# Attention of a hybrid decoder step: exponentials split in two as the stationary side, their remainders computed by POOL

## The chip, the core and the metric

One core of one Trainium2 chip runs the whole program. The metric is the device time of one execution in microseconds (us).

## The reference

The program is one inference step of a two-layer decoder, for a prompt of 2048 rows and for 8 decode rows with 4096 rows of paged cache each. All of it is fp32. Layer 0 (gated MLP and a linear recurrence) is not touched by the change. Layer 1 is forgetting attention with 16 heads of 64:

```python
q, k_p, v_p, g, logf_p = _fox_project(yp, norm1_g, w_in1, fox_b_f, q_norm_g, k_norm_g)
att = _fox_prompt_attention(q, k_p, v_p, logf_p)
yp = yp + (att * jax.nn.silu(g)) @ w_out1
...
s = jnp.einsum('bqhd,bkhd->bhqk', q_i, k) * ATTN_SCALE
s = s + cq_i[..., :, None] - ck[:, :, None, :]
p = jax.nn.softmax(jnp.where(mask, s, -jnp.inf), axis=-1)
return jnp.einsum('bhqk,bkhd->bqhd', p, v)
```

`_fox_sample_attention` does the same for the decode rows over the paged keys and values.

## The kernel before

The program is a row of stages: setup, norm and layer 0 (to about 745 us), the output projection of layer 0, `project1` (about 1024 to 1880), `past`, `attention` (about 1921 to 3225) and `out1` (from about 3239). In each stage every engine has its own instruction list, and semaphores tie them together. An F32R matmul is PE's one-pass form of fp32 and sees a rounded operand; a product that must keep fp32 is made of a rounded high part and the remainder, in three such matmuls (`split3`, L112 to L114).

**`project1`** makes q, k, v and g of the prompt in 128 units (16 column chunks of 256 in the order q, k, v, g, times 8 row pairs; `unit`, 48 matmuls of 256 columns). q and k are squared on ACT (L1373), normed on DVE (L1541, for k also L1549) and transposed by PE (`turn`, L1241, four 128x128 per unit), since attention wants them by feature; g goes through Silu and is transposed too. `turn(n - 1)` stands behind `unit(n)` in PE's list. v and k also go to DRAM by rows. Beside that POOL and DVE make the scores of the decode rows with the paged keys (L1151, L1564; `p_kp` a page, `p_qb` the query row spread over partitions).

**`attention`** works by units: a head times a chunk of 512 queries, c = 0 to 3. Unit c has 4(c+1) blocks of 128 keys; a block is a *step*, 40 steps a head, 640 in all. A Python function, `schedule`, writes the order; the loop body is a pair of heads, one decode row's attention rides on each pair. The kinds of work in that order are:

- `M` (L1953, on the diagonal L1956): one product of 128 queries by up to 512 keys, rounded, into one of two PSUM banks; DVE takes its row maxima (L2076). `MN` (L2080) joins them, `MR` (L1963) turns them into a row by four transposes, and ACT writes that row into Q2 (L2046), where it acts as the 65th feature.
- `QK`: the scores of one step, 128 keys by up to 512 queries, as two matmuls (L1975 with high and low parts of q stacked, L1977) and the mask on the diagonal (L1980). ACT takes the exponential into `W` (L2040).
- `PV` (L1990), two steps behind: `V` (128 keys by 65, the last column ones) is stationary and `W` moves, in fp32, into one bank `O` of 65 by 512.
- `OE`: DVE multiplies `O` by the gate (L2086), ACT copies the 65th row, the sum of the exponentials (L2051), and POOL stores both (L1920, L1922); the sum is divided out only in `out1`.
- `SD` to `VC`: the decode row. `SD` (L2092, L2093) begins it; `VG` (L2016) are eight groups of four V pages, on the odd head of each pair, the pages loaded by SP two groups ahead.
- `LD`: ten loads of the next head; a memset on POOL (L1929) puts the ones row into Q2.

PE's waits around the change read, in the order of a step:

```python
pe.wait_ge(ex, NS * i + max(0, n - 1))
...
pe.wait_ge(ex, NS * i + n + 1)
if kb == 0:
    pe.wait_ge(oed, 2 * NC * i + u)
    pe.wait_ge(oea, 2 * NC * i + u)
nc.tensor.matmul(O[0:HR, P * j:512], V[s][:, kb, :], W[n % 3][:, 0:512 - P * j],
```

**`out1`** multiplies 17 tiles of rows with the output weights by `split3`. For each tile it inverts the sums, spreads them over the features of each head by 16 matmuls (L2282) and multiplies (L2239) before it splits the result (L2215, L2246).

Of the kernel before, what the change touches and what calls it, by code (L numbers as in the profile page):

```python
# [965 lines left out]
def project1(nc, z, a, C, xh, xl, D, out):  # L966
# [22 lines left out]
    def turn_no(n):  # L989
        return count("qkg", n)  # L990
# [4 lines left out]
    def rows_stored(n):  # L995

        return 16 * slots("kv", n, lambda m: m)
# [14 lines left out]
    with ExitStack() as ctx:  # L1012
# [57 lines left out]
        def _(sp):  # L1070
# [66 lines left out]
            for x in range(2):  # L1137
                sp.wait_ge(scst[x], 16 * (B // 2))
                sp.wait_ge(hst[x], 16 * (count("qkg", N) // 2))
                sp.wait_ge(lst[x], 16 * (count("qk", N) // 2))  # L1140
                sp.wait_ge(rst[x], 16 * (count("kv", N) // 2))
# [12 lines left out]
        def _(pe):  # L1154
# [67 lines left out]
            def turn(n):  # L1222
# [4 lines left out]
                elif kind == "k":  # L1227
                    pe.wait_ge(kgained, count("k", n + 1))
                else:
                    pe.wait_ge(vfree, count("vg", n + 1))  # L1230
                if x >= 2:
                    pe.wait_ge(hid, x - 1)
                    before = [m for m in range(n) if UNITS[m][2] in "qkg" and turn_no(m) == x - 2][0]
                    pe.wait_ge(lod, low_no(before + 1))
# [19 lines left out]
            for n in range(N):  # L1254
# [9 lines left out]
            turn(N - 1)  # L1264

        @block.scalar
        def _(act):
# [22 lines left out]
            def hi(n):  # L1290
# [4 lines left out]
                if kind == "g":  # L1295
                    nc.scalar.activation(hi_t[:, x % 2].bitcast(F32), tp[x % 2][:], ACT.Copy).then_inc(hid, 1)
                else:
                    nc.scalar.activation(hi_t[:, x % 2], tp[x % 2][:], ACT.Copy, scale=C.qg[:] if kind == "q" else 1.0).then_inc(hid, 1)

            def store_hi(n):  # L1300
# [4 lines left out]
                dst = {"q": D.qh, "k": D.kh, "g": D.sg}[kind]  # L1305
# [12 lines left out]
            def store_rows(n):  # L1318
# [4 lines left out]
                else:  # L1323
                    act.wait_ge(vfree, count("vg", n + 1))
                act.dma_start(out[kind + "_prompt"][0, CWD * u:CWD * u + CWD, HC * i:HC * i + HC, :].rearrange("(t r) h d -> r t (h d)", r=P),
                              rows[:, n % 2]).then_inc(rst[n % 2], 16)
# [37 lines left out]
            for n in range(N):  # L1364
                c, u, kind = UNITS[n]
                if n >= 2 and UNITS[n - 2][2] in "qk":
                    store_lo(n - 2)
                if n and UNITS[n - 1][2] in "kv":
# [10 lines left out]
                if n and UNITS[n - 1][2] != "v":  # L1379
                    hi(n - 1)  # L1380
# [3 lines left out]
                if n and UNITS[n - 1][2] != "v":  # L1384
                    store_hi(n - 1)
# [3 lines left out]
            hi(N - 1)  # L1389
            store_hi(N - 1)  # L1390

        @block.vector
        def _(dve):
# [130 lines left out]
            for n in range(N):  # L1524
# [5 lines left out]
                if n and UNITS[n - 1][2] in "qk":  # L1530
                    lo(n - 1)
# [138 lines left out]

# [720 lines left out]
```

## Time and profile before

| | us |
|---|---|
| median of 3 runs (lowest to highest) | 3478.22 (3470.8 to 3479.21) |
| the profiled execution, its own time | 3480.33 |
| its span, first to last instruction | 3478.7 |
| PE busy | 3017.1 (87%) |
| DVE busy | 1533.7 (44%) |
| ACT busy | 1032.3 (30%) |
| POOL busy | 761.5 (22%) |
| mean granted TensorE clock, share of full speed | 0.935 |
| DMA | 547.04 MB in 323904 packets |

The profile is one execution. An engine's busy time is the sum of its instructions; PE's matmuls are pipelined and their ends modelled, so starts are safer to read than ends. "Idle before" is what an engine stood still ahead of an instruction, and behind the arrow stands what released it. Lines are those of the kernel before.

### The profile page before, as it was taken

To read this page: it belongs to the slowest core of one execution; us is meant where nothing else is said; L and a number is where in the kernel's file an instruction comes from. 1 tells how busy PE (TensorE), PEld (TensorE's weight loads), DVE (VectorE), ACT (ScalarE), POOL (GpSimd) and SP (SyncE) were. 2 spreads that over 40 slices of the span, in tenths; PEclk is the share of its full clock that TensorE was granted. 3 is DMA by queue.
4 is the path that set the end of the run, shared out by engine and by line. 5 is a ranking of instruction groups with operands and counts; after the bars stand their busy time and mean duration, and the time that the engine had idled before them with its cause. 6 is when DMAs were issued, how large, how long until landed. Compare 5 with 4: busy or idle time off the path is not lost. (4 is left out here: it accounts for less than half of the span.)

```text
span 3478.7 us, 48124 instructions
## 1 busy us (share of the span) xinstructions
PE 3017.1 (87%) x17005; PEld 2320.1 (67%) x17005; DVE 1533.7 (44%) x2068; ACT 1032.3 (30%) x1711; POOL 761.5 (22%) x475
## 2 busy tenths in 40 slices
PE   3879797959989999989996689898989889899799
PEld 3869696947759999989886445454545445454687
DVE  5132323233557667685775334343424333342332
ACT  5222223232452122221211234343434343343100
POOL 0000000010004886878765200000100000000000
PEclk9989898979989999999998799999999999999899
DMA  3111000035636888888785765748475757654442
GB/s 113 32 35 39 25 30 25 24 101 178 184 115 210 271 267 276 265 260 269 252 271 159 167 183 137 205 114 250 99 228 127 215 150 200 173 143 152 149 127 68
DMA packets 323904, 547.04 MB, mean 157 GB/s; under 512 B 77309, under 2 KB 221345, under 8 KB 314220
## 3 DMA queue, kind: packets, MB, share of 16 engines
q1 hardware_dynamic: 220172, 445.81, 42.8%
q10 hardware_dynamic: 95424, 75.61, 7.6%
q0 software_dynamic: 8128, 23.33, 2.1%
q8 instruction: 98, 1.61, 0.2%
q14 instruction: 82, 0.67, 0.1%
HBM read 449.58 MB, written 95.12 MB: 157 GB/s over the span
## 5 line engine op out<-in xcount | busy, mean ns | idle before, releaser
L1151 POOL TENSOR_TENSOR p_kp<-p_kp,p_qb 128x1024 f32<-128x1024 f32 x256 | 625.7, 2471 | 385.7 <-DMA p_kp<-in_cache_k_dram 314.0
L2076 DVE TENSOR_REDUCE at_mx<-at_mx 128x1 f32<-128x512 f32 (+3 forms) x640 | 379.9, 608 | 718.3 <-PE at_mx L1953 475.7
L2040 ACT ACTIVATE at_w<-at_st,c_nckt 128x512 f32<-128x512 f32 (+3 forms) x640 | 397.3, 623 | 690.9 <-PE at_st L1977 380.2
L1990 PE MATMUL at_o<-at_w,at_v 128*65 128x512 f32 (+3 forms) x1280 | 578.0, 535 | 17.0 <-DVE at_og L2086 8.0
L112 PE MATMUL p_pb<-p_w,x_xh 128*128 128x256 f32 x2048 | 591.8, 289 | 0.7 <-DVE p_w L1462 0.7
L113 PE MATMUL p_pb<-p_w,x_xh 128*128 128x256 f32 x2048 | 579.1, 283 | 0.0
L114 PE MATMUL p_pb<-p_w,x_xl 128*128 128x256 f32 x2048 | 578.6, 283 | 0.0
L1975 PE MATMUL at_st<-at_q,at_k 128*128 128x512 f32 (+3 forms) x640 | 407.4, 637 | 4.4 <-ACT at_w L2040 4.4
L1564 DVE TENSOR_REDUCE p_sc<-p_kp 128x16 f32<-128x1024 f32 x256 | 307.5, 1214 | 217.6 <-POOL p_kp L1151 217.3
L112 PEld LDWEIGHTS p_pb<-p_w,x_xh 128*128 128x128 f32 x2048 | 390.5, 191 | 12.1 <-issue 11.2
L113 PEld LDWEIGHTS p_pb<-p_w,x_xh 128*128 128x128 f32 x2048 | 391.9, 191 | 0.0
L114 PEld LDWEIGHTS p_pb<-p_w,x_xl 128*128 128x128 f32 x2048 | 391.2, 191 | 0.0
L112 PE MATMUL l_pb<-x_xh,l_wh 128*128 128x412 f32 x800 | 289.1, 361 | 73.1 <-DVE l_wl L857 73.1
L1920 POOL DMA_DIRECT2D att<-at_og x64 | 34.5, 539 | 1187.2 <-DVE at_og L2086 928.8
L113 PE MATMUL l_pb<-x_xl,l_wh 128*128 128x412 f32 x800 | 285.8, 357 | 0.0
L114 PE MATMUL l_pb<-x_xh,l_wl 128*128 128x412 f32 x800 | 285.3, 357 | 0.0
L1953 PE MATMUL at_mx<-at_km,at_q 65*128 65x512 f32 (+3 forms) x640 | 245.5, 402 | 35.5 <-DMA at_k<-kl 29.8
L112 PE MATMUL o_pp<-o_wh,o_mh 128*128 128x512 f32 (+1 forms) x544 | 220.7, 406 | 33.1 <-DVE o_wl L586 22.7
L1975 PEld LDWEIGHTS at_st<-at_q,at_k 128*128 128x128 f32 x640 | 122.9, 192 | 179.1 <-issue 152.9
L1977 PE MATMUL at_st<-at_q,at_k 65*128 65x512 f32 (+3 forms) x640 | 237.5, 371 | 0.0
L2016 PE MATMUL at_cv<-at_vp,at_sw 128*32 128x512 f32 x1056 | 154.1, 663 | 82.9 <-DMA at_vp<-in_cache_v_dram 82.9
L113 PE MATMUL o_pp<-o_wl,o_mh 128*128 128x512 f32 (+1 forms) x544 | 216.2, 397 | 0.0
(289 smaller groups left out, 3880.4 us busy)
## 6 DMA issues: line engine op xcount, KB each, us to landing
p_kp<-in_cache_k_dram SPq DMA_DIRECT2D x256, 512.0 KB, 4.9
at_vp<-in_cache_v_dram SPq DMA_DIRECT2D x256, 512.0 KB, 5.6
o_mt<-mixed SPq DMA_DIRECT2D x32, 512.0 KB, 5.1
p_raw<-in_w_in_dram SPq DMA_DIRECT2D x32, 512.0 KB, 6.9
at_q<-qh SPq DMA_DIRECT2D x32, 512.0 KB
at_k<-kh SPq DMA_DIRECT2D x32, 512.0 KB
l_raw<-in_w_in_dram SPq DMA_DIRECT2D x20, 512.0 KB
mixed<-l_w POOLq DMA_DIRECT2D x8, 1028.0 KB, 4.2
```

Source lines behind the costliest of these rows:

```text
L112: nc.tensor.matmul(out, lhs[0], rhs[0], start=(k == 0), stop=False)
L113: nc.tensor.matmul(out, lhs[0], rhs[1], start=False, stop=False)
L114: return nc.tensor.matmul(out, lhs[1], rhs[0], start=False, stop=(k == nk - 1))
L1151: nc.gpsimd.tensor_tensor(kp[:, g % 4], kp[:, g % 4], qb[:], ALU.mult).then_inc(kmul, 1)
L1564: nc.vector.tensor_reduce(sc[:, b % 2].rearrange("p (h g) -> p h g", g=z.PG)[:, :, r], by_head(kp[:, g % 4], z.H), AX.X, ALU.add).then_inc ...
L1953: last = nc.tensor.matmul(MX[m % 2][:, 0:wd], Q2[s][0:HR, t * P:(t + 1) * P], KM[s][0:HR, seg * 512:seg * 512 + wd], start=True, stop=seg < c)
L1975: nc.tensor.matmul(ST[n % 2][:, 0:wd], K1[s][:, ks], Q1[s][:, q0:q0 + wd], start=True, stop=False)
L1977: last = nc.tensor.matmul(ST[n % 2][:, 0:wd], K2[s][:, ks], Q2[s][:, q0:q0 + wd], start=False, stop=not diagonal)
L1990: nc.tensor.matmul(O[0:HR, P * j:512], V[s][:, kb, :], W[n % 3][:, 0:512 - P * j], start=(kb == 0), stop=(kb == 4 * c + 3)).then_inc(pv, 1)
L2016: last = nc.tensor.matmul(CV[32 * g:32 * g + 32, half, :], sw[:, 4 * r + g, :], src[:, 512 * half:512 * half + 512], start=(r == 0), stop= ...
L2040: nc.scalar.activation(W[n % 3][:, 0:wd], ST[n % 2][:, 0:wd], ACT.Exp, bias=C.nckt[:, kb, ds(2 * i + u // NC, 1)]).then_inc(ex, 1)
L2076: nc.vector.reduce_max(mx[:, u % 2, j, seg:seg + 1], MX[m % 2][:, 0:wd], AX.X).then_inc(mread, 1)
```

## The change

1. `project1`: g is stored by rows like k and v, without transposes. The transposes of q and k stand two units behind the products, not one, and with them ACT's high part, DVE's low part and their stores.
2. `attention` is written out in full, with no loop over pairs. The exponentials `W` are rounded by ACT into `Wh` (step kind `RD`), and POOL computes every remainder `Wl` = `W` - `Wh` (`WL`; `low_on_dve` is always false). For each 128 queries `Wh` and then `Wl` are the stationary side, and V moves: 130 columns (high part 64, ones 2, low part 64) for `Wh`, 66 for `Wl`. `O` is now 128 queries by 2 banks of 260 columns, opened by a matmul with zeros. `PV` is three steps behind, and held for two steps at the start of a unit. V is split once a head, high part on ACT, low part on POOL (`VS`). `MR` uses a bank of the two of `M`. `OE` comes in two halves, after the PV of block 4c+1 and of the last: DVE inverts the sum, scales by it and the gate, and adds the two parts. The gate is loaded and the result stored for each unit, by rows, on SP's queue.
3. `out1`: the sums, their inverses, the 16 matmuls and the multiply go; each tile is turned by 8 transposes.

```diff
@@ project1 @@
-                if n and UNITS[n - 1][2] != "v":
-                    turn(n - 1)
+                if n >= 2 and UNITS[n - 2][2] in "qk":
+                    turn(n - 2)
...
@@ attention, the order @@
+                if n >= 2:
+                    seq.append(("WL", n - 2))
+                pending.append((u, kb, n))
+                if hold:
+                    hold -= 1
+                while len(pending) > LAG and not (hold and pending[0][1] == 0):
+                    p = pending.pop(0)
+                    weigh(p)
+                    if p[1] == blocks(p[0]) - 1:
+                        hold = 2
...
@@ attention, PE @@
-                        nc.tensor.matmul(O[0:HR, P * j:512], V[s][:, kb, :], W[n % 3][:, 0:512 - P * j],
-                                         start=(kb == 0), stop=(kb == 4 * c + 3)).then_inc(pv, 1)
...
+                    for jj in range(j, 4):
+                        if kb == 0 and u and jj % 2 == 0:
+                            pe.wait_ge(osc, 2 * u - 1 + jj // 2)
+                        if kb == 0 and jj % 2 == 0:
+                            nc.tensor.matmul(O[:, jj // 2, 0:2 * VW], identr[0:1, :], zero[:], start=True, stop=False)
+                        q = slice(P * (jj - j), P * (jj - j + 1))
+                        nc.tensor.matmul(o_tile(jj, ALL), Wh[n % RH][:, q], V[s][:, kb, ALL], start=False, stop=False)
+                        last = nc.tensor.matmul(o_tile(jj, FRONT), Wl[n % RH][:, q], V[s][:, kb, FRONT], start=False,
+                                                stop=jj % 2 == 1 and kb == 4 * c + jj)
...
@@ attention, ACT @@
+            value_high(0)
+            value_high(1)
...
+                elif w[0] == "RD":
+                    n = w[1]
+                    wd = width(n)
+                    act.wait_ge(ex, n + 1)
+                    if n >= RH:
+                        act.wait_ge(pv, n - RH + 1)
+                    nc.scalar.activation(Wh[n % RH][:, 0:wd], W[n % RW][:, 0:wd], ACT.Copy).then_inc(rdd, 1)
...
@@ attention, POOL @@
+                if w[0] == "WL" and not low_on_dve(w[1]):
+                    n = w[1]
+                    wd = width(n)
+                    pool.wait_ge(rdd, n + 1)
+                    nc.gpsimd.tensor_tensor(Wl[n % RH][:, 0:wd], W[n % RW][:, 0:wd], Wh[n % RH][:, 0:wd].bitcast(F32), ALU.subtract).then_inc(wlp, 1)
...
@@ attention, DVE @@
-                        nc.vector.tensor_tensor(og[u % 2][0:HD, :], O[0:HD, :], SG[s][:, 512 * c:512 * c + 512], ALU.mult).then_inc(oed, 1)
...
+                    nc.vector.reciprocal(ol[:, u % 2, 2 * half:2 * half + 2], one).then_inc(old, 1)
...
+                    for part, dst in ((HI, oa), (LO, ob)):
+                        for j in js:
+                            last = nc.vector.scalar_tensor_tensor(out=dst[:, j, :], in0=o_tile(j, part), scalar=ol[:, u % 2, j:j + 1],
+                                                                  in1=SG[u % 2][:, j, :], op0=ALU.mult, op1=ALU.mult)
+                    last.then_inc(osc, 1)
...
+                    nc.vector.tensor_tensor(og[u % 2][:, 2 * half:2 * half + 2, :], oa[:, 2 * half:2 * half + 2, :],
+                                            ob[:, 2 * half:2 * half + 2, :], ALU.add).then_inc(oadd, 1)
...
@@ out1, PE @@
-                    last = nc.tensor.matmul(rb[:, n % 2, k, 0:rows], expand[:, k * P:(k + 1) * P], rl[:, ds(col, rows)],
-                                            start=True, stop=True)
+                    last = nc.tensor.transpose(tp[:, n % 2, k, :], mt[:, n % 3, k * P:(k + 1) * P], C.ident[:])
```

How the order of the instructions moves, first on PE at the end of a short unit (`at_st` scores, `at_mx` products for maxima, `at_o` the output). Before:

```order
L1990 MATMUL at_o<-at_w,at_v 65x256
L1975 MATMUL at_st<-at_q_0,at_k_0 128x512
L1977 MATMUL at_st<-at_q_0,at_k_0 128x512
L1953 MATMUL at_mx<-at_km,at_q_0 128x512 x2
L1956 MATMUL at_mx<-at_maskr,at_identr 128x128
L1990 MATMUL at_o<-at_w,at_v 65x128
```

After, from the last PV but one of the unit:

```order
L2063 MATMUL at_o<-at_v,at_wh 128x130
L2064 MATMUL at_o<-at_v,at_wl 128x66
L2039 MATMUL at_st<-at_q_0,at_k_0 128x512
L2041 MATMUL at_st<-at_q_0,at_k_0 128x512
L2017 MATMUL at_mx<-at_km,at_q_0 128x384
L2020 MATMUL at_mx<-at_maskr,at_identr 128x128
L2039 MATMUL at_st<-at_q_0,at_k_0 128x512
L2041 MATMUL at_st<-at_q_0,at_k_0 128x512
L2017 MATMUL at_mx<-at_km,at_q_0 128x512
L2061 MATMUL at_o<-at_zero,at_identr 128x260
```

Between the last PV of a unit and the first of the next there are now two QKs and no PV; the matmul with zeros opens the new sum. On DVE, at the start of a head (`at_mx` the maxima, `at_sd` the decode row's scores, `at_o` the output), before:

```order
L2092 TENSOR_TENSOR at_sd<-at_sc,c_decay 128x16x32
L2093 ISA
L2093 TENSOR_TENSOR at_sd<-at_sn,c_decay 128x16
L2075 REGISTER_ALU
L2076 TENSOR_REDUCE at_mx<-at_mx 128x1
```

and after:

```order
L2148 TENSOR_REDUCE at_mx<-at_mx 128x1 x2
L2186 TENSOR_TENSOR at_sd<-at_sc,c_decay 128x16x32
L2187 TENSOR_TENSOR at_sd<-at_sn,c_decay 128x16
L2148 TENSOR_REDUCE at_mx<-at_mx 128x1 x2
L2166 RECIPROCAL at_ol<-at_o 128x2
L2172 SCALAR_TENSOR_TENSOR at_oa<-at_o,at_ol,at_sg 128x64 x2
L2172 SCALAR_TENSOR_TENSOR at_ob<-at_o,at_ol,at_sg 128x64 x2
L2178 TENSOR_TENSOR at_og<-at_oa,at_ob 128x128
```

Where one multiply per unit stood in DVE's list among four or more reduces, there is now, twice per unit, a reciprocal, four scaled multiplies and an add.

## Rows read from the trace of the kernel before

**Rows 1.** Windows of the span: project1 and attention; the first line names the columns.
```profile
core 0: us, PE busy (x) PEld busy (x) DVE busy (x) ACT busy (x) POOL busy (x), PEclk, DMA share, GB/s
1037.00:1880.00 843.00, 799.10 (x6671) 779.22 (x6670) 576.15 (x657) 189.18 (x334) 625.72 (x256) 0.97 0.80 256
1960.00:3224.00 1264.00, 1153.94 (x5167) 626.35 (x5165) 469.06 (x850) 481.82 (x776) 90.69 (x140) 0.95 0.61 169
```

**Rows 2.** Timeline of PE in a full step: start, us, engine, line, operation.
```profile
2501.31 0.79 PE L1975 MATMUL at_st<-at_q,at_k 128*128 128x512 f32 x1
2502.17 1.02 PE L1990 MATMUL at_o<-at_w,at_v 128*65 128x512 f32 x2
2502.63 0.80 PE L1975 MATMUL at_st<-at_q,at_k 128*128 128x512 f32 x1
```

**Rows 3.** The same windows for one pair of heads; 2123.8 begins the even head.
```profile
2123.80:2142.40 18.60, 17.55 (x66) 11.05 (x64) 12.04 (x22) 7.25 (x12) 3.87 (x5) 0.82 0.70 162
2124.00:2194.00 70.00, 68.26 (x284) 40.67 (x284) 33.44 (x62) 31.96 (x52) 5.95 (x9) 0.95 0.38 84
2128.00:2133.00 5.00, 5.00 (x13) 2.76 (x12) 2.53 (x6) 0.37 (x1) 0.52 (x1) 0.50 0.65 154
2194.00:2287.00 93.00, 79.73 (x371) 39.58 (x370) 26.56 (x48) 28.65 (x47) 5.95 (x9) 0.93 0.81 234
```

**Rows 4.** Costliest groups of the page, the V pages of the decode rows.
```profile
L2016 PE MATMUL at_cv<-at_vp,at_sw 128*32 128x512 f32 x1056 | 154.1, 663 | 82.9 <-DMA at_vp<-in_cache_v_dram 82.9
```

**Rows 5.** Groups of attention by line and form: ACT's exponential, DVE's reduce.
```profile
L2040 ACT ACTIVATE at_w<-at_st,c_nckt 128x512 f32<-128x512 f32 x448 | 307.0, 687 | 501.2 <-PE at_st L1977 380.2 <-PE at_st L1980 74.3 <-issue 44.6
L2076 DVE TENSOR_REDUCE at_mx<-at_mx 128x1 f32<-128x512 f32 x448 | 302.6, 687 | 518.0 <-PE at_mx L1953 475.7 <-PE at_mx L1956 41.9
```

**Rows 6.** Timeline of PE in project1, one unit's four transposes.
```profile
1870.13 0.60 PE L1241 MATMUL p_tp<-c_ident,p_rows 128*128 128x128 f32 x4
1870.48 0.36 PE L112 MATMUL p_pb<-p_w,x_xh 128*128 128x256 f32 x1
1870.69 0.28 PE L113 MATMUL p_pb<-p_w,x_xh 128*128 128x256 f32 x1
1870.81 0.28 PE L114 MATMUL p_pb<-p_w,x_xl 128*128 128x256 f32 x1
```

**Rows 7.** The transposes' line L1241 in project1: what ended PE's idle time, us, times.
```profile
  DVE p_rows L1541: 45.8, 10
  DVE p_rows L1549: 33.0, 25
```

**Rows 8.** Timeline of project1 at the longest of these waits, in brackets idle time and releaser.
```profile
1481.21 2.34 POOL L1151 TENSOR_TENSOR p_kp<-p_kp,p_qb 128x1024 f32<-128x1024 f32 x1 [11.70 <-DMA p_qb<-qs]
1486.95 1.11 PE L1241 MATMUL p_tp<-c_ident,p_rows 128*128 128x128 f32 x4 [10.29 <-DVE p_rows L1541]
```

**Rows 9.** Chain that ended last, one tile of out1.
```profile
3265.94 1.98 PE o_rb L2282 x16
```

**Rows 10.** Timeline at the start of attention, ACT's first exponential.
```profile
1961.66 1.28 ACT L2040 ACT_TABLE_LOAD   x1 [0.41 <-PE at_st L1980]
```

**Rows 11.** Timeline of PE, sixteen loads with one column each.
```profile
3217.50 1.84 PE L2023 MATMUL at_cv<-c_onescol,at_cm 128*128 128x1 f32 x16
```

**Rows 12.** POOL's lines L1151 and L1929: duration ns min/median/max.
```profile
L1151 POOL TENSOR_TENSOR p_kp<-p_kp,p_qb x256: 2337/2397/3426, 1046.8 to 1871.0; 128x1024 f32<-128x1024 f32 x128
L1929 POOL MEMSET at_q<- x14: 1797/1799/1801, 2031.9 to 3086.7; 1x2048 f32 x14
```

**Rows 13.** ACT's rounding copy of 128x512 in out1, L2225.
```profile
L2225 ACT ACTIVATE o_wh<-o_raw x16: 612/630/634, 3245.4 to 3258.6; 128x512 fp32r<-128x512 f32 x16
```

**Rows 14.** DVE's lines L1541 (from PSUM), L1549 (from SBUF), and four small ones.
```profile
L1541 DVE TENSOR_TENSOR p_rows<-p_pb,p_rs x64: 690/691/693, 1040.7 to 1781.5; 128x512 f32<-128x512 f32 x64
L1549 DVE TENSOR_TENSOR p_rows<-p_rows,p_kgb x32: 691/1098/2896, 1092.2 to 1782.2; 128x512 f32<-128x512 f32 x32
20.31 1.01 DVE L201 TENSOR_SCALAR c_w<-c_ident,su_w 8x8 f32<-8x8 f32 x4
```

More of the change, by code:

```diff
@@ L1680, in attention, with blocks, first_step, width @@
     HR = HD + 1
-    NS = 2 * sum(4 * (c + 1) for c in range(NC))
-    NLD = 10
+    U = H * NC
+    HB = 2 * (NC * (NC + 1))
+    N = HB * H
+    NLD = 8
     VG = PG // 4
-    VI = PG // 4 + 1
+    VW = 2 * HD + 2
+    LAG = 3
+    RW, RH = 4, 5
+    def blocks(u):
+        return 4 * (u % NC + 1)
+    def first_step(u):
+        return HB * (u // NC) + sum(blocks(x) for x in range(u % NC))
+    def width(n):
+        u = max(x for x in range(NC * (n // HB), NC * (n // HB) + NC) if first_step(x) <= n)
+        kb = n - first_step(u)
+        return 512 - P * max(0, kb - 4 * (u % NC))
@@ L1685, in attention @@
+    SEQ = schedule()
+    RING = [w for w in SEQ if w[0] in ("M", "MR")]
     with ExitStack() as ctx:
@@ L1875, in _ @@
-            run(0, schedule(False), True, False)
-            with sp.Fori(1, B - 1) as i:
-                run(i, schedule(False), False, False)
-            run(B - 1, schedule(True), False, True)
+            due = []
+            for w in SEQ:
+                if w[0] == "LD":
+                    head_load(w[1], w[2])
+                elif w[0] == "LV":
+                    value_load(w[1])
+                elif w[0] == "OE" and w[2] == 1:
+                    due.append([3, w[1]])
+                elif w[0] == "SD" and w[-1] < B - 1:
+                    sp.wait_ge(sdd, 2 * w[-1] + 2)
+                    scores(w[-1] + 1)
+                elif w[0] == "VG":
+                    values(w[-1], w[1])
+                elif w[0] == "VN":
+                    values(w[-1], VG)
+                elif w[0] == "QK":
+                    for d in due:
+                        d[0] -= 1
+                    while due and due[0][0] <= 0:
+                        u = due.pop(0)[1]
+                        store(u)
+                        if u + 2 < U:
+                            gate_load(u + 2)
@@ L1880, in _ @@
+            for _, u in due:
+                store(u)
             sp.wait_ge(fin, 2)
-            sp.dma_start(D.att[:, T:TS].rearrange("(k p) b -> p k b", p=P), atts[:]).then_inc(fst, 16)
-            sp.dma_start(D.lsum[:, T:TS], ones[:]).then_inc(fst, 16)
-            sp.wait_ge(fst, 32)
+            sp.dma_start(D.atts.rearrange("(k p) b -> p k b", p=P), atts[:]).then_inc(fst, 16)
+            sp.wait_ge(fst, 16)
+            for x in range(2):
+                sp.wait_ge(ogst[x], 16 * (U // 2))
@@ L1885, in _ @@
         @block.gpsimd
         def _(pool):
-            nc.gpsimd.memset(sw[:], 0.0).then_inc(made, 1)
+            for s in range(2):
+                nc.gpsimd.memset(K2[s][HD:HR].bitcast(F32), 1.0).then_inc(made, 1)
+                nc.gpsimd.memset(Q2[s][HD:HR].bitcast(F32), 1.0).then_inc(onesd, 1)
+            pool.wait_ge(made, 2)
+            pool.wait_ge(onesd, 2)
+            nc.gpsimd.memset(zero[:].bitcast(F32), 0.0).then_inc(made, 1)
+            pool.wait_ge(made, 3)
             nc.gpsimd.memset(sn[:], 0.0).then_inc(snz, 1)
@@ L2159, in out1, with by_feature @@
         block = ctx.enter_context(nc.Block())
+        def by_feature(n, rows):
+            return tp[:, n % 2, :, :] if rows == P else ms[:]
         @block.sync
```

770 lines of the change are left out of this document (390 added, 380 removed).

## The prediction

> **What bounds the kernel now.** I read the table of windows first. Attention, from 1960 to 3224 us, is 1264 us of the span, and PE is busy in 1154 of them, DVE in 469, ACT in 482 and POOL in 91 [rows 1]: PE is the engine that the others feed. Its timeline shows a full step without a product as QK, QK, PV, one step every 1.32 us (2501.31 to 2502.63) [rows 2]. 256 columns take 0.12 us in a dense stretch [rows 6], so the two score matmuls of 512 columns take 0.43 to 0.48 and leave about 0.87 to PV's 512 columns in fp32, which is four cycles a column at 2.4 GHz. PE has no gap there. The windows of one pair of heads say where it has: the even head takes 70 us (2124 to 2194), the odd one 93 us [rows 3]; the odd one holds the V pages of the decode rows, where PE sat 82.9 us idle over all eight pairs until pages landed [rows 4]. The first eight steps of the even head take 18.6 us, 5 of them at a clock of 0.50, the 1.2 GHz level, after PE had stopped again and again for DVE's reduces [rows 3]. ACT and DVE need 687 ns each for a 128x512 piece, half a step [rows 5].
>
> **`project1`.** The gate's units are no longer transposed: 32 units of four transposes go. The timeline has four of them at 1870.13 and the products behind them at 1870.48, 1870.69 and 1870.81; products are 0.12 apart otherwise, so they took 0.35 + 0.09, say 0.45 us per unit [rows 6], and 32 x 0.45 = 14.4 us. The other part is the lag. Transposes of q and k now stand two units behind instead of one. PE sat idle 45.8 and 33.0 us, 79 together, before transposes until DVE's normed rows were there [rows 7]. One more unit is 48 matmuls x 0.118 = 5.7 us of cover. That covers all of the short waits; the longest is 10.29 us, from a query row that landed late (POOL waited 11.70 us for it, DVE waits for POOL, PE for DVE) [rows 8], and keeps some 4.6 us. Some waits also move to the next thing that DVE is late with, since its work is the same: of 79 I take 43, with ends of 16 and 79. The sum is -57, ends -30 and -93. The order of the loads and stores moves by one unit of 5.7 us and nothing waits for the gate's stores; that is priced at nothing.
>
> **`out1`.** Sixteen expand matmuls per tile take 1.98 us on the chain, 15 times alike, and more at the first tile [rows 9]. Eight 128x128 transposes take their place: at 0.11 a piece 0.9, say 0.98. 16 x 1.0 = 16, and 2 more for the reciprocals and the divide ahead of the first tile: -18, ends -12 and -20.
>
> **Start of attention.** ACT now rounds V of heads 0 and 1 ahead of its first exponential, and V(1) stands on SP's queue behind about 12.5 MB. Before, ACT turned to its first exponential at 1961.66 [rows 10]. From about 1920, 12.5 MB at 256 GB/s end at 1969, at 169 GB/s at 1994 [rows 1]. With the first QK waiting for ACT's maxima row too, this is +15, ends +3 and +35.
>
> **Attention, PE.** Per 128x128 block of weights there are now two loads and matmuls of 130 and 66 columns. Sixteen loads with a single column took 1.84 us, 0.115 each [rows 11]; that is load-bound, and 130 or 66 columns fit under it. 2 x 2176 of them plus 128 zeroing ones, at 0.111 (between 0.107, 256 columns' time, and that 0.115), are 497 us. What goes is 278,528 columns x 4 cycles = 464 us. So PE gains nothing from one-pass arithmetic: +33, ends +15 and +51.
>
> **Attention, POOL.** 640 remainders. No row has a 512-wide one; nearest is the two-input TENSOR_TENSOR of 128x1024 at 2337 ns [rows 12]: half is 1.17, the whole 2.34. I take 1.3. A head is then 28 x 1.3 + 4 x (1.0 + 0.7 + 0.4) + 4.2 = 49 us, under its PE work (58); at 2.34 it would be 84 a head and POOL the bound. The chain exponential 0.69, rounding 0.63 [rows 5, 13], remainder 1.3 and 0.3 of semaphores is 2.9 us, and a lag of three steps gives 4.5: hidden in full steps. Once a head POOL also splits V's low part (2.4 us, the row's own price for 1024 elements) while ACT rounds the high part (1.1): 3.5, less the 1.6 of slack, is 1.9 x 14 = +27, ends 0 and +49. The memset of the ones row (1.80 us [rows 12]) stands before the first steps' remainders and is covered: POOL is ahead there, since DVE holds the start; without that cover it costs 25.
>
> **Attention, DVE.** It gives up one multiply per unit and gets two halves of an evacuation: a reciprocal 0.16, four scaled multiplies 128x64 at 0.23 (four small ones follow each other in 1.01 us [rows 14]), a wait on itself 0.1, an add of two SBUF tiles 0.3, and 0.4 for what POOL does to such an add: a DVE add from PSUM took 690 to 693 ns whatever POOL did, one from SBUF 691 to 2896 with a median of 1098 [rows 14]. 1.9 each, 128 of them. Where does that matter? In the first eight steps of a head sixteen reduces (10.0) and four halves are 17.6 us against 10.8 before; 18.6 passed there with DVE busy in 12.0 [rows 3]. Between 0 (it fits the 6.6 idle) and 6.8 (in series) I take 5, because reduces and PE's products alternate on two banks: 16 x 5 = +80, ends 0 and +109. At the change to units c=2 and c=3, four steps hold 6.3 and 5.8 us of DVE against 3.9 and 4.3 of PE, so +3.9 x 16 = +62, ends 0 and +62. The queued reduces wait behind the halves, and PE waits for both: its next products, and its first PV into O.
>
> **What absorbs it.** The 82.9 us of page waits [rows 4] are in the odd heads; a slower head gives pages time. About half of what I add lies there, (33 + 27 + 80 + 62)/2 = 101, more than the waits, so most of them go, but not all lie where the delay does: -70, ends 0 and -83. Attention nets 33 + 27 + 80 + 62 - 70 = +132.
>
> **Sum.** 3480.3 of the profiled execution (2 above the median of the runs, inside their spread) - 57 - 18 + 15 + 132 = 3552.3.
>
> **Rivals.** *Everything new is hidden.* DVE's halves fit its idle time, POOL keeps ahead: what remains is PE's 33 with half absorbed and a start of 3. 3480 - 57 - 18 + 3 + 17 = 3425. For it: DVE is busy in 37% of attention [rows 1]. Against: the start of a head, where that share was 12.0 of 18.6. *Near cancel*: half of the new waits, 3480. *The clock falls.* In the first steps of a head it was 0.50 for 5 us [rows 3]; with more stops there and at unit changes the mean of attention could go from 0.95 to 0.85: 65 us a head x (1/0.85 - 1/0.95 = 0.124) = 8, x 15 to 16 heads = +120: 3672. It decides from when PE's stops double.
>
> *Loads in series.* If a short matmul did not cover the next load, each of the 2176 pairs would cost its 196 columns, 0.0815 us, more: +177, 3729. The rows speak against: pairs of a 128-wide load and 256 columns follow each other 0.12 us apart [rows 6], less than load plus matmul. The Trainium skill, page "TensorE: Matmul & The Clock Gate", Part 3, "What overlaps and what doesn't", says that a load overlaps a matmul in flight only where their row groups differ, which here they don't. By that rule this rival would be the forecast; the trace disagrees with its 0.12.
>
> **How the numbers follow.** Chances: the forecast 0.54, all hidden 0.26, near cancel 0.05, clock 0.12, loads in series 0.03. A measurement of this kernel can tell about 0.3%, 10 us. Faster comes from the hidden case, same from the cancel, slower from the rest. Range: the hidden case with a better lag (-20) to the clock case and the forecast with its DVE and PE terms at their upper ends (3552 + 29 + 18 + 22 + 20 for the start, 3641), so 3405 to 3700; the forecast's own range is 3500 to 3640.
>
> **What would show it.** In the profile after: in `project1` no idle before transposes but one of some 5 us, and 1880 turned into about 1823; POOL's 128x512 remainder near 1.3 us and never the releaser for long; in attention, PE's PV matmuls 0.111 apart; DVE's halves near 1.9 us, with PE idle until DVE's scaled tiles and maxima were there, some 5 us at each head start and 2 at unit changes; L2016's counterpart with 10 us of idle instead of 83; 0.98 per tile in `out1`. I am wrong if attention takes under 1270 us (hidden), if POOL's remainders end the waits before PV, which means they cost well over 1.5 us, or if PV pairs are 0.19 apart.

## The result, and the profile after

The change takes 4024.21 us in the median of 4 runs (4013.81 to 4033.41) against 3477.53: a ratio of 1.1575, interval 1.1536 to 1.1615. The forecast was 3552 with 3405 to 3700. The sign was right, the size was not, and the reason given for the size was the wrong one. A time of a whole kernel that stands below without a range in brackets is of one run. One stage with the same code in it differs a little from kernel to kernel: `project1` by up to 10 us, attention by up to 21 of 1820.

The page after, its first and second parts (the engines' busy time; PEclk is the granted clock in tenths, 40 slices of the span):

```profile
span 4031.8 us, 54111 instructions
PE 3607.7 (89%) x19933; PEld 3102.5 (77%) x19933; DVE 1633.7 (41%) x2738; ACT 1280.0 (32%) x2271; POOL 1433.6 (36%) x1000
PEclk6989889799999999998557575766758576665799
```

The mean clock of the whole execution fell from 0.935 to 0.791, and nearly all of that lies in the slices of attention. The windows of the kernel after answer to [rows 1]: `project1` from first to last product, attention from the first exponential to the last PV, and what follows.

```profile
core 0: us, PE busy (x) PEld busy (x) DVE busy (x) ACT busy (x) POOL busy (x), PEclk, DMA share, GB/s
1027.40:1882.90 855.50, 795.75 (x6602) 776.10 (x6601) 580.86 (x670) 179.23 (x313) 624.66 (x256) 0.96 0.78 252
1991.00:3808.90 1817.90, 1776.35 (x8359) 1436.74 (x8358) 601.66 (x1547) 743.39 (x1364) 763.07 (x668) 0.65 0.43 115
3808.90:4031.80 222.90, 203.22 (x946) 164.47 (x945) 52.79 (x60) 26.11 (x33) 0.00 (x0) 0.94 0.39 134
```

The same cuts of the kernel before, from its instructions' first and last starts:

| stretch | before, us | after, us | difference | forecast |
|---|---|---|---|---|
| up to `project1`'s first product | 1023.5 | 1027.4 | +3.9 | 0 |
| `project1` | 852.6 | 855.5 | +2.9 | -57 |
| last product to first exponential | 86.9 | 108.1 | +21.2 | +15 |
| attention | 1260.2 | 1817.9 | +557.7 | +132 |
| last PV to the end | 255.5 | 222.9 | -32.6 | -18 |
| span | 3478.7 | 4031.8 | +553.1 | +72 |

Attention holds it all. At full clock its 1817.9 us would be 1817.9 x 0.65 = 1182, and the 1260.2 of before 1260.2 x 0.95 = 1197: in clock cycles the stage is no longer than before. PE's own work in it is a little more, 1776.35 x 0.65 = 1155 against some 1153.94 x 0.95 = 1096 [rows 1], and PE stands still less. Its waits in attention after, in us in total, times and longest:

```profile
PE at_cv L2089 <- DMA at_vp<-in_cache_v_dram: 31.9, 9, 6.2
PE at_mx L2017 <- DVE at_mx L2148: 4.0, 12, 0.5
PE at_mx L2027 <- DVE at_mx L2148: 3.2, 16, 0.2
PE at_o L2063 <- POOL at_wl L1981: 1.2, 7, 0.2
```

That is 40 us. Before, PE was idle for 110 (1264.00 less 1153.94 [rows 1]), 82.9 of them for pages [rows 4]. What changed is how many columns PE streams while it is busy. Windows of two stretches of the kernel after show PE busy with hardly a gap at either clock:

```profile
2500.00:2560.00 60.00, 60.00 (x242) 54.71 (x240) 13.71 (x33) 25.75 (x46) 26.26 (x23) 0.50 0.02 5
2650.00:2660.00 10.00, 9.84 (x79) 9.00 (x77) 2.05 (x3) 7.57 (x13) 8.07 (x7) 1.00 0.57 197
```

PE's timeline at full clock, then at the lower one, 1.2 GHz (start, us, engine, line, operation):

```profile
2656.25 0.31 PE L2063 MATMUL at_o<-at_v,at_wh 128*128 128x130 f32 x1
2656.39 0.24 PE L2064 MATMUL at_o<-at_v,at_wl 128*128 128x66 f32 x1
2656.47 0.31 PE L2063 MATMUL at_o<-at_v,at_wh 128*128 128x130 f32 x1
...
2695.14 0.46 PE L2063 MATMUL at_o<-at_v,at_wh 128*128 128x130 f32 x1
2695.39 0.36 PE L2064 MATMUL at_o<-at_v,at_wl 128*128 128x66 f32 x1
2695.57 0.46 PE L2063 MATMUL at_o<-at_v,at_wh 128*128 128x130 f32 x1
```

A pair of PV matmuls takes 0.22 us at full clock and 0.43 at half. 0.22 us is 528 cycles at 2.4 GHz, and it streams 130 + 66 = 196 columns. Before, PV's 512 columns in fp32 took about 0.87 us of a step [rows 2], and four cycles for each column are 0.85 of that: hardly a cycle was left over. And where does the clock come back? Here, with 512 columns under each load of 32:

```profile
2560.41 0.36 PE L2064 MATMUL at_o<-at_v,at_wl 128*128 128x66 f32 x1
2560.71 3.64 PE L2089 MATMUL at_cv<-at_vp,at_sw 128*32 128x512 f32 x16
...
2566.01 0.24 PE L2064 MATMUL at_o<-at_v,at_wl 128*128 128x66 f32 x1
2566.09 0.31 PE L2063 MATMUL at_o<-at_v,at_wh 128*128 128x130 f32 x1
```

The clock had been 0.50 since 2500 and before; behind sixteen V-page matmuls it is full. (Sixteen times 512 columns would be 6.8 us at 1.2 GHz one after another, and they took 3.6: these matmuls, 32 output rows each, partly run side by side.) It fell again at 2661 (0.51 in the mean from 2660 to 2700), behind the sixteen one-column matmuls of a decode row and a step of 384 columns. This repeats. Seven times the clock falls behind these sixteen matmuls and stays down through the whole next even head, which has no V pages, until the first V pages of the odd one (once until the second group). Two of the seven stretches:

```profile
2435.80:2565.30 129.50, 129.32 (x496) 112.58 (x495) 39.31 (x102) 49.29 (x91) 51.25 (x45) 0.50 0.21 43
2661.10:2790.60 129.50, 129.32 (x498) 112.76 (x498) 40.43 (x102) 49.70 (x92) 51.19 (x45) 0.50 0.21 43
```

Together the seven are 917 us, 915 of them PE busy, out of 1282 that attention spends at the lower level. The kernel before has the same sixteen one-column matmuls [rows 11], and in its attention no stretch at the lower level is longer than 14 us. That gave **theory 1**, columns streamed, against **theory 2**, that PE's stops for ACT, POOL and DVE bring the clock down, which was the mechanism of my own rival.

### The profile page after: what moved, and what is told of

It is laid out like the page before. It is cut to its first block and busy times, and to the rows that moved or that the text cites. A ratio compares the mean times of both kernels' runs of the same rounds, so it can differ in the third digit from the quotient of the medians.

```text
span 4031.8 us, 54111 instructions
## 1 busy us (share of the span) xinstructions
PE 3607.7 (89%) x19933; PEld 3102.5 (77%) x19933; DVE 1633.7 (41%) x2738; ACT 1280.0 (32%) x2271; POOL 1433.6 (36%) x1000
## 5 line engine op out<-in xcount | busy, mean ns | idle before, releaser
L1981 POOL TENSOR_TENSOR at_wl<-at_w,at_wh 128x512 fp32r<-128x512 f32 (+3 forms) x640 | 708.1, 1110 | 1025.6 <-ACT at_wh L2126 1023.3
L1151 POOL TENSOR_TENSOR p_kp<-p_kp,p_qb 128x1024 f32<-128x1024 f32 x256 | 624.7, 2466 | 388.0 <-DMA p_kp<-in_cache_k_dram 312.0
L2063 PE MATMUL at_o<-at_v,at_wh 128*128 128x130 f32 x2176 | 747.0, 379 | 1.2 <-POOL at_wl L1981 1.2
L2064 PE MATMUL at_o<-at_v,at_wl 128*128 128x66 f32 x2176 | 674.2, 316 | 0.0
L2063 PEld LDWEIGHTS at_o<-at_v,at_wh 128*128 128x128 f32 x2176 | 598.0, 275 | 50.2 <-issue 15.1
L2064 PEld LDWEIGHTS at_o<-at_v,at_wl 128*128 128x128 f32 x2176 | 602.6, 277 | 19.8
L2039 PE MATMUL at_st<-at_q,at_k 128*128 128x512 f32 (+3 forms) x640 | 385.3, 602 | 0.1
L2017 PE MATMUL at_mx<-at_km,at_q 65*128 65x512 f32 (+3 forms) x640 | 316.5, 523 | 58.8 <-ACT at_q L2131 30.8
L2126 ACT ACTIVATE at_wh<-at_w 128x512 fp32r<-128x512 f32 (+3 forms) x640 | 355.6, 556 | 0.0
L2041 PE MATMUL at_st<-at_q,at_k 65*128 65x512 f32 (+3 forms) x640 | 314.4, 491 | 0.0
```

Of the source, the lines that this page charges most:

```text
L1151: nc.gpsimd.tensor_tensor(kp[:, g % 4], kp[:, g % 4], qb[:], ALU.mult).then_inc(kmul, 1)
L1981: nc.gpsimd.tensor_tensor(Wl[n % RH][:, 0:wd], W[n % RW][:, 0:wd], Wh[n % RH][:, 0:wd].bitcast(F32), ALU.subtract).then_inc(wlp, 1)
L2017: last = nc.tensor.matmul(MX[r % 2][:, 0:wd], Q2[s][0:HR, t * P:(t + 1) * P], KM[s][0:HR, seg * 512:seg * 512 + wd], start=True, stop=seg < c)
L2039: nc.tensor.matmul(ST[n % 2][:, 0:wd], K1[s][:, ks], Q1[s][:, q0:q0 + wd], start=True, stop=False)
L2063: nc.tensor.matmul(o_tile(jj, ALL), Wh[n % RH][:, q], V[s][:, kb, ALL], start=False, stop=False)
L2064: last = nc.tensor.matmul(o_tile(jj, FRONT), Wl[n % RH][:, q], V[s][:, kb, FRONT], start=False, stop=jj % 2 == 1 and kb == 4 * c + jj)
```

## The experiments

**Columns against stops.** `wl130` moves all 130 columns of V for the remainders as well:

```diff
-                        last = nc.tensor.matmul(o_tile(jj, FRONT), Wl[n % RH][:, q], V[s][:, kb, FRONT], start=False,
+                        last = nc.tensor.matmul(o_tile(jj, ALL), Wl[n % RH][:, q], V[s][:, kb, ALL], start=False,
```

> The change, but the remainders move all 130 columns of V instead of 66 (their product with V's low part is added; it is tiny). Theory 1: what costs is the clock, and it falls because a pair of weight loads now streams only 196 columns. With 260 per pair the clock in attention rises somewhat, from 0.65 to 0.70 or more, and the time falls below 3950 us. Theory 2: the clock falls because PE stops for ACT, POOL and DVE (the new chain behind each exponential, the longer evacuation). Then the padding changes nothing: 4000 to 4050 us, clock 0.65.

4010.23 us (3997.72 to 4018.72), ratio 1.1535 (1.1498 to 1.1572). Attention 1794.6 us at 0.67. The time lies in the range that theory 2 had set, its interval overlaps that of the change, and the clock is in the direction of theory 1 but below its 0.70. Alone it settles nothing. `pad256` moves 256 columns under every load:

```diff
+        WIDE = slice(0, 256)
+        flat = [Vx[s][:].rearrange("p k n -> p (k n)") for s in range(2)]
...
-                        nc.tensor.matmul(o_tile(jj, ALL), Wh[n % RH][:, q], V[s][:, kb, ALL], start=False, stop=False)
+                        nc.tensor.matmul(o_tile(jj, WIDE), Wh[n % RH][:, q], flat[s][:, kb * VW:kb * VW + 256], start=False, stop=False)
```

> The change, but both matmuls of a pair move 256 columns of V (the columns behind the 130 are the next block's and land in unused columns of O; 256 columns take about as long as the load behind them, so PE's work stays nearly the same at a given clock). Theory 1 (columns): the clock in attention comes back to 0.9 or more and the time to 3450 to 3600 us. Theory 2 (stops of PE): clock and time stay as in the change, 4000 us or more.

3656.37 us (3641.49 to 3670.67), ratio 1.0516 (1.0472 to 1.0559). The same instructions, more streamed, and 368 us less. Its window of attention:

```profile
1988.20:3431.40 1443.20, 1346.67 (x8360) 1053.34 (x8358) 599.09 (x1544) 738.59 (x1365) 764.74 (x668) 0.93 0.53 145
```

The clock, 0.93, is as theory 1 expected; the time is 56 us above its 3450 to 3600. Theory 2 is out by this alone: ACT, POOL and DVE have the same work, and PE even stands still longer than in the change (96.5 us, 55 of them for V pages, against 41.6) at the higher clock. The counterproof takes a link of the chain away and leaves the columns (`no_remainder`; the remainders and their part of the output are left out):

```diff
-                        last = nc.tensor.matmul(o_tile(jj, FRONT), Wl[n % RH][:, q], V[s][:, kb, FRONT], start=False,
+                        last = nc.tensor.matmul(o_tile(jj, FRONT), Wh[n % RH][:, q], V[s][:, kb, FRONT], start=False,
...
-                if n >= 2:
-                    seq.append(("WL", n - 2))
```

> The change without POOL's remainders: the second matmul of each pair takes the rounded exponential again, with its 66 columns, so PE's list and its columns are the same, but nothing waits for POOL (the remainders and what they add to the output are left out). Theory 1: the clock stays at 0.65 and the time within 40 us of 4024. Theory 2, or a theory by which POOL is the bound: under 3800 us.

4005.87 us; attention:

```profile
1986.30:3782.00 1795.70, 1760.22 (x8358) 1426.05 (x8358) 580.85 (x1546) 743.22 (x1364) 55.63 (x28) 0.65 0.42 116
```

Of POOL's 763 us of work 56 are left, and the clock is 0.65 as in the change: at this clock POOL is neither the bound nor the cause.

**How the clock follows the columns.** `pad192` is `pad256` with 192 in place of 256.

> The change with 192 columns for every PV matmul, between wl130 (260 columns per pair, attention 1795 us at a clock of 0.67) and pad256 (512 per pair, 1443 us at 0.93). PE's time for a pair at full clock should be the loads' in all three. If the clock follows the columns gradually, attention lies midway, 1550 to 1700 us at 0.75 to 0.88. If it needs nearly full use of the columns, it stays above 1750; if 384 per pair are already enough, it is under 1450 us, and the whole below pad256's 3656, since less is streamed.

3816.52 us (3806.31 to 3832.90), ratio 1.0964 (1.0925 to 1.1004):

```profile
1987.70:3609.10 1621.40, 1531.17 (x8358) 1215.73 (x8358) 597.05 (x1546) 740.88 (x1364) 763.59 (x668) 0.78 0.48 129
```

So it is gradual, as the first case had it: 196, 260, 384 and 512 columns per pair give a mean clock of 0.65, 0.67, 0.78 and 0.93 and 1818, 1795, 1621 and 1443 us. These are means over a stage whose clock jumps between its two levels, and they do not follow the columns evenly: the first 64 added columns hardly move them. The stretches at the lower level say why. Seven of about 130 us stand in the change, in `no_remainder` and in `wl130` alike; in `pad192` the seven are 58 to 89 us, and in `pad256` the longest is 24.

**What attention would cost at the clock of before.** `pad256_no_remainder` joins the two edits above.

> 256 columns for every PV matmul and no remainders by POOL (the rounded exponential moves twice, the remainders' part is left out). With the clock at 0.93, attention still took 1443 us against 1260 before. If POOL's link in the chain is what is left, it falls by 50 us or more here; if it is DVE's evacuation and PE's own columns, it stays within 25 us of 1443.

3599.88 us, attention 1392.8 at 0.95: 50 us less than `pad256`, at the edge of what had been set for POOL's link. PE's waits for POOL were only 11.2 us there, and the clock's step from 0.93 to 0.95 is worth 1443.2 x 0.02 / 0.95 = 30, so part of the 50 comes by way of the clock. `pad256_light_evacuation` makes each half of the evacuation one copy (the division, the gate and the low part are left out):

```diff
-                    nc.vector.reciprocal(ol[:, u % 2, 2 * half:2 * half + 2], one).then_inc(old, 1)
...
+                    nc.vector.tensor_copy(og[u % 2][:, 2 * half:2 * half + 2, :],
+                                          O[:, half, 0:512].rearrange("p (j n) -> p j n", n=256)[:, :, 0:HD]).then_inc(osc, 1)
```

> 256 columns for every PV matmul, and each half of the evacuation is one copy by DVE (the division by the sum, the gate and the addition of the low part are left out). Attention took 1443 us with the whole evacuation and 1393 without POOL's remainders. If the halves delay PE at head starts and unit changes by what the prediction said (142 us, less what page waits absorb), attention falls to 1300 to 1370 us; if DVE's idle time held them, it stays above 1420.

3618.9 us, attention 1405.3, again at 0.95. That is 38 us less than in `pad256`, some of it again by the clock, and lies between the two expectations: the halves cost something, but far less than 142; that DVE's idle time holds the rest is the likely reading, not a shown one. In the kernel after, one half stands in DVE's timeline so:

```profile
2632.26 0.16 DVE L2166 RECIPROCAL at_ol<-at_o 128x2 f32<-128x2 f32 x1
2632.52 0.47 DVE L2172 SCALAR_TENSOR_TENSOR at_oa<-at_o,at_ol,at_sg 128x64 f32<-128x64 f32 x2
2632.92 0.46 DVE L2172 SCALAR_TENSOR_TENSOR at_ob<-at_o,at_ol,at_sg 128x64 f32<-128x64 f32 x2
2633.48 0.29 DVE L2178 TENSOR_TENSOR at_og<-at_oa,at_ob 128x128 f32<-128x128 f32 x1
2633.69 0.28 DVE L2148 TENSOR_REDUCE at_mx<-at_mx 128x1 f32<-128x128 f32 x1
```

1.43 us from the reciprocal to the next reduce, where I had 1.9.

One cost of PE's own was sized wrong. The matmuls with zeros that open a sum, two per unit, had been priced like a load, 0.111 us. At full clock the start behind one comes 0.31 us later:

```profile
2638.01 0.38 PE L2061 MATMUL at_o<-at_zero,at_identr 1*128 1x260 f32 x1
2638.32 0.33 PE L2063 MATMUL at_o<-at_v,at_wh 128*128 128x130 f32 x1
```

**`project1`.** `lag_one` puts the transposes of q and k, and what hangs on them on ACT and DVE, back to one unit:

```diff
-                if n >= 2 and UNITS[n - 2][2] in "qk":
-                    turn(n - 2)
+                if n and UNITS[n - 1][2] in "qk":
+                    turn(n - 1)
```

> The change with the transposes of q and k in project1 one unit behind the products again instead of two. If the lag of two gave 43 us, project1 (first to last product, 855 us in the change) takes 880 to 900. If project1 is paced by its loads, as the unchanged 852 and 855 us before and after suggest, it takes 850 to 860 again, and PE's idle time only moves from one wait to another.

4047.58 us; `project1` 861.6. With the lag of two it takes 855.5 in the change and 847.5 to 857.5 in the kernels made from it with full pages, so the lag is worth 4 to 14 us, hardly more than these differ among themselves, and not 43. The first reason why 43 was out of reach lies in the rows that the forecast went by. The 45.8 and 33.0 us of [rows 7] are the sum over two engine lists, the matmuls (PE) and their weight loads (PEld), which stand in the same waits. PE's own before are half of that:

```profile
PE p_tp L1241 <- DVE p_rows L1541: 22.4, 5, 10.3
PE p_tp L1241 <- DVE p_rows L1549: 15.2, 12, 3.7
PE p_sm L1178 <- DMA p_raw<-in_w_in_dram: 3.2, 2, 2.1
PE p_pb L112 <- DVE p_w L1462: 0.7, 1, 0.7
```

PE's waits in the kernel after, from 1100 on:

```profile
PE p_sm L1178 <- DMA p_raw<-in_w_in_dram: 19.2, 2, 10.6
PE p_tp L1238 <- DVE p_rows L1537: 14.0, 4, 7.5
PE p_pb L112 <- DVE p_w L1458: 10.8, 6, 5.5
PE p_tp L1238 <- DVE p_rows L1545: 9.5, 7, 2.1
```

The waits for normed rows fell from 37.6 to 23.5 us, and waits for the next chunk's weights rose from 3.9 to 30.0 (`p_raw` is loaded, `p_w` split). PE's idle time in `project1` grew from 47.6 to 59.8 us, which took back the 9.3 by which it was busy for less. Who is it that paces? Two pairs of kernels take work from the decode scores. Half of each K page behind the first four (the scores of the other rows are left out; in the second kernel of the pair V of head 1 is also split later):

```diff
+                rows_in = P if g < 4 else P // 2
+                sp.dma_start(kp[0:rows_in, g % 4], a["cache_k"][ds(r, 1), 0:rows_in].rearrange("o p h d -> p (o h d)")).then_inc(k_in[g % 4], 16)
...
-        loads = {}
+        loads = {20: [("VS", 1)]}
```

> The kernel before, but each of project1's K pages behind the first four is loaded by half (64 of 128 rows, so the decode rows' scores over the rest are left out). Theory P1: project1 is paced by its loads (852 us and 250 to 253 GB/s in every version so far). Then it gets clearly shorter, 810 us or less. Theory P2: it is paced by the chain from its products through DVE to the transposes; then it stays at 845 to 855 us.

> The change with the same half K pages and, in another stage, V of head 1 split at step 20 instead of before ACT's first exponential. Project1: by P1 the change's saving (14 us of gate transposes, 43 of waits) now shows, and project1 is 30 to 60 us shorter than in the kernel before with half pages; if it is again within 5 us of that kernel, something else than the loads takes it back. Start of attention: if ACT's wait for V of head 1 is what made the way from project1's last product to the first exponential 108 us instead of 87, it falls to 84 to 92.

`project1` takes 825.0 us before and 831.0 after (3439.19 and 3968.16 us in all). Neither expectation holds for the first: 27 us less is between the two. Nor does either for the second: it was to be 30 to 60 us shorter, or within 5, and is 6 longer, with 19.5 us of waits for `p_raw`. So with half the bytes something still takes the change's saving back. The start of attention is plain: from the last product to the first exponential 77.3 us in place of 108.1, even less than the 84 to 92 set. The lighter pages are not why, since `light_pages_after`, below, with them and with V of head 1 in its place, has 108.0. ACT had stood there behind V of head 1, as its timeline in the kernel after shows:

```profile
1948.25 1.06 ACT L2105 ACTIVATE at_v<-at_vr 128x1024 fp32r<-128x1024 f32 x1 [64.44 <-DMA at_vr<-out_v_prompt_dram]
1980.33 1.06 ACT L2105 ACTIVATE at_v<-at_vr 128x1024 fp32r<-128x1024 f32 x1 [31.01 <-DMA at_vr<-out_v_prompt_dram]
```

The second pair loads and multiplies one head of each page only, with DVE's reduces in full (the other heads' scores are left out):

```diff
+                nw = z.D if g < 4 else z.HD
+                nc.gpsimd.tensor_tensor(kp[:, g % 4, 0:nw], kp[:, g % 4, 0:nw], qb[:, 0:nw], ALU.mult).then_inc(kmul, 1)
```

> The kernel before, but behind the first four K pages project1 loads only one head of each page (32 KB for 512) and POOL multiplies only that head; DVE's reduce stays in full, the other decode scores are left out. With half the bytes project1 fell from 852 to 825 us. If loads and POOL paced the rest too, it falls to 800 us or less; if DVE's list does, it stays at 820 to 825.

> The change with the same light K pages. In the prediction the lag of two units and the missing gate transposes save 57 us of PE's time in project1. If POOL and the loads are what takes that back, project1 is now at least 20 us shorter than in light_pages_before. If it is not, the saving is taken back inside the chain of DVE, ACT and the weights of the next column chunk, and it never was one.

3417.91 and 3952.7 us in all. Windows of `project1`, before and then after:

```profile
1026.90:1828.20 801.30, 790.66 (x6722) 775.27 (x6722) 521.68 (x670) 194.84 (x343) 98.60 (x256) 0.99 0.37 114
```

```profile
1026.60:1808.80 782.20, 776.03 (x6602) 761.63 (x6601) 524.18 (x670) 178.94 (x313) 95.12 (x256) 0.99 0.38 117
```

The kernel before is at 801.3, where 800 or less had been set for loads and POOL as the pace. And now the change saves 19.1 us, just short of the 20 that was set: PE is busy for 14.6 less, which is the gate's transposes, and idle for 4.5 less. So the saving of the transposes comes through when PE is the bound (99% busy in both windows). With the pages in full, about 850 us is what the page work (loads and POOL) and its effects allow, and PE's saving comes out as waits elsewhere. Which link does it, the transfers, POOL's multiplies or the weights queued behind the pages, these runs do not part: loads by half gave 27 us, loads and POOL together 51.

**A version that beats both.** `v_stationary` keeps the split of the exponentials but turns PV round (`project1`, `out1` and the gate as in the kernel before; the rounding of a head's last eight steps goes to DVE):

```diff
+                    nc.tensor.matmul(O[0:HD + 2, u % 2, P * j:512], V[s][:, kb, 0:HD + 2], Wh[n % RH][:, 0:wd], start=(kb == 0), stop=False)
+                    nc.tensor.matmul(O[0:HD, u % 2, P * j:512], V[s][:, kb, LO], Wh[n % RH][:, 0:wd], start=False, stop=False)
+                    nc.tensor.matmul(O[0:HD + 2, u % 2, P * j:512], V[s][:, kb, 0:HD + 2], Wl[n % RH][:, 0:wd], start=False,
+                                     stop=(kb == 4 * c + 3)).then_inc(pv, 1)
```

> A version meant to beat both. The exponentials are split as in the change (rounded part, remainder by POOL), but V's high part with ones and V's low part are stationary and the exponentials move, three one-pass matmuls of up to 512 columns per step (high x high, low V x high, high V x remainder) in place of one four-pass one; output by features, evacuated by one multiply on DVE that takes the row of sums along, two banks for it; rounding of the last eight steps of a head on DVE; project1, out1 and the gate as before the change. PE's work per full step is 5 x 512 columns instead of 6 x 512: 116 us less. Theory 1 (columns hold the clock): clock 0.93 or more in attention, which takes 1130 to 1250 us, and 3350 to 3480 us in all. If splitting itself lowers the clock, or the chain of exponential, rounding and remainder is the limit, attention takes more than 1300 us.

3455.85 us (3443.68 to 3470.65), ratio 0.9926 (0.9890 to 0.9962): 0.7% faster than before, small but outside the noise, attention at a clock of 0.94. The upper end of the expectation is 1250, and it took 1249.2; PE waited 94.5 us for pages and 33 for POOL in it. `v_stationary_spread` moves the page groups apart and PV one step further back (against `v_stationary`):

```diff
-                a0, a1 = (len(side) * n) // N, (len(side) * (n + 1)) // N
-                seq += side[a0:a1]
+                b, step = divmod(n, 2 * HB)
+                seq += [(*w, b) for w, at in zip(tail, PLACE) if at == step]
...
+        PLACE = [2 * x for x in range(10)] + [20 + 7 * x for x in range(VG)] + [72, 73, 76, 79]
```

> v_stationary with two moves: the eight groups of V pages of a decode row stand seven steps apart over the pair of heads instead of three or four apart in its second half, and PV is four steps behind instead of three. PE waited 94.5 us for pages and 33 for POOL's remainders there. If both go, attention falls from 1249 to 1130 to 1180 us and the whole to 3340 to 3400. If the clock gives it back or the exponentials on ACT (685 us) are the next bound, it stays above 3420.

3345.21 us (3344.15 to 3351.35), ratio 0.9632 (0.9601 to 0.9663); attention's window, and PE's longest waits in it:

```profile
1958.70:3099.00 1140.30, 1063.06 (x5799) 702.39 (x5798) 563.90 (x977) 679.54 (x1237) 765.24 (x669) 0.95 0.68 188
```

```profile
PE at_mx L2032 <- DMA at_k<-kl: 54.2, 7, 8.5
PE at_o L2072 <- POOL at_wl L1996: 10.2, 7, 1.5
```

Is that the pages alone? `spread_before` has the kernel before with only that order:

```diff
-                    a0, a1 = (len(side) * (n - 1)) // NS, (len(side) * n) // NS
-                    seq += [w for unit in side[a0:a1] for w in unit]
+                    seq += [w for w, at in zip(tail, PLACE) if at == n - 1]
```

> The kernel before with nothing but the groups of V pages spread over the pair of heads, as in v_stationary_spread (attention 1140 us). PE waited 82.9 us for pages there. If the pages were all, attention falls from 1260 to about 1180 and the whole to 3390 to 3420 us, and the one-pass arithmetic with V stationary is worth what is left, 40 to 80 us. If PE's four passes leave the page work no room, it stays above 3440.

3472.94 us (3469.03 to 3481.90), ratio 0.9997 (0.9981 to 1.0014): nothing. Attention takes 1252.4 us, where 1180 had been set for the pages being all. The page waits are gone, and PE waits for the next head's keys instead, which stand behind the pages in the queue:

```profile
PE at_mx L1952 <- DMA at_k<-kl: 75.3, 7, 14.0
```

Spreading alone gains nothing, and one-pass arithmetic with what `v_stationary` brings along 0.7%; together, with the longer lag, 3.7%. How much of the 3.7% is the lag was not tried.

## Why the prediction was wrong, point by point

- **The clock** (the rival "the clock falls"). The forecast kept 0.95 in attention, the rival 0.85 at a chance of 0.12; it was 0.65. Of the 558 us in attention, 375 are the clock's by the step from 1818 to 1443 in `pad256`. The step that failed is in "Attention, PE": 130 or 66 columns "fit under" the load, so the forecast priced them by time alone and left the clock at 0.95, a term put at nothing. They are free in time at full clock, but PE streams 196 columns in 528 cycles, and with these the clock was 0.65; with 512 it was 0.93. The rival had the clock, but its mechanism was wrong as well: "with more stops there and at unit changes", and "decides from when PE's stops double". PE's idle time went down, from 110 us to 42. The row of 5 us at 0.50 in [rows 3] I laid to stops; that row has PE busy in 5.00 of 5.00 us, and in the 4 us ahead of it the two waits for DVE are 0.16 and 0.20.
- **Attention, PE**: 0.111 us per load, forecast and measured at full clock (0.22 a pair). The 128 opening matmuls took 0.31 and not 0.111, which is 26 us more than priced, so the term was nearer its upper end, +51, than +33. "PE gains nothing from one-pass arithmetic" held for this form; with V stationary it gains.
- **Loads in series**: out, as forecast. By the forecast's own figures a load, a matmul of 130, a load and one of 66 columns would be 0.30 us in series, and they took 0.22. The Trainium skill's page "TensorE: Matmul & The Clock Gate", Part 3, "What overlaps and what doesn't", lets a load overlap a matmul in flight only where their row groups differ. Here they don't, and the 0.22 disagrees.
- **POOL**: a remainder was forecast at 1.3 us and took 1.27 (x441); V's low part 2.4, measured 2.17. The lag hid it as said: PE waited 1.2 us for it in the change. The +27 is not shown either way. With the clock restored PE waited 11.2 us for POOL, and leaving the remainders out (V's split stays in) gave 50, some 30 by the clock.
- **DVE**: +142, less what page waits absorb. The half was 1.43 us, not 1.9, because the add took 0.29 to 0.41 and not 0.7, and what the halves do beyond one copy was 38 us at a restored clock. The lower end was the better one.
- **Attention without the clock**: the net +132 compares with +183 in `pad256`. In that lie its clock (0.93 for 0.95, some 30 us) and its padded pairs (0.24 us in place of 0.22, some 40). That leaves about +110, an estimate: without the fall of the clock the forecast would have been close, in part by luck, since terms that were too large (DVE) and too small (the opening matmuls) met.
- **`project1`**: -57, measured +3. The 14.4 us are real (PE is busy for 14.6 less with light pages), but they show only where PE is the bound. Two steps failed. The 79 us of waits were a misreading: PE's own were 37.6, so the 43 that I took were more than there was to have. And waits of PE behind DVE are no saving when the page work and the weights behind them set the pace: those for rows fell by 14.1 us and those for weights rose by 26.1.
- **Start**: +15 forecast, +21 measured, by the named mechanism, as the later split of V in `half_pages_after` shows.
- **`out1`**: -18, measured -33. Transposes take 0.87 us where I had 0.98, and the way to the first product shortened from 29 to 20 us, where I had 2. Some 5 us of the 33 stay unaccounted for.
- The page waits fell to 31.9 us and not to 10. With the clock restored they were 55.0.

The Trainium skill, page "TensorE: Matmul & The Clock Gate", section "Why this matters for your kernels", says to keep TensorE busy without gaps between bursts to hold the full clock. The trace here disagrees for this kind of work: PE busy in 60.00 of 60 us at 0.50.

## What to carry to other kernels

A matmul that hides under its weight load is free only as long as the clock stays. When a change turns a long moving side into short ones, count the columns streamed per cycle before and after, not only PE's busy time, and prefer the operand order that moves the long side. An engine's wait is a saving only where the next thing in its way isn't set by the same slow neighbour. And before waits are added up, see whether a matmul's wait and that of its weight load are one and the same.

## What the runs showed of the hardware

- PE can be fully busy and stay at the 1.2 GHz level: 60.00 of 60 us at 0.50, and 129.32 of 129.50, with PV pairs of 196 columns in 0.43 us. The mean clock of attention went 0.65, 0.67, 0.78, 0.93 with 196, 260, 384 and 512 columns per pair of loads.
- In the change each of the seven long stretches at the lower level began behind sixteen matmuls of one column and ended behind a group of V-page matmuls of 512 columns, with no idle time of PE just ahead of either.
- Two 128-wide weight loads and 196 columns take 0.22 us at 2.4 GHz: the loads run beside the matmuls, though both use all 128 rows.
- A matmul of one row by 260 columns that opens a sum held the next start back by 0.31 us at full clock.
- Padding matmuls with columns that nobody reads made the kernel 368 us faster.
